# RG-LRU layer: input parts taken before the norm's root, the root multiplied in by VectorE as units leave PSUM

## The chip, the cores and the metric

The kernel runs on one core of a Trainium2 chip. The metric is the device time of one execution in microseconds (us). Engine names as in the profile: PE is TensorE's matmul, PEld its weight load, DVE VectorE, ACT ScalarE, POOL GpSimd, SP the engine that issues the DMAs.

## The reference, cut to what matters

The model has four layers: latent attention, HGRN2, RG-LRU, latent attention. Every layer computes `x + W_out(mixer(in_proj(rmsnorm(x))) * silu(gate))`. The change concerns the third layer and the norm in front of it:

```python
def rmsnorm(x, g):
    y = xf * lax.rsqrt(jnp.mean(xf * xf, axis=-1, keepdims=True) + EPS)
    return (y * g).astype(x.dtype)

def rglru_layer(h, conv_buf, h0, w_in, conv_w, conv_b, w_a, b_a, w_x, b_x, lam, w_out):
    xb, gate = jnp.split(h @ w_in, 2, axis=-1)
    y = conv_b + sum(xpad[:, j:j + s] * conv_w[j] for j in range(C_CONV))   # causal, width 4
    r = sigmoid(yh @ w_a + b_a);  i = sigmoid(yh @ w_x + b_x)               # per head, 128x128
    log_a = -C_GATE_C * r * softplus(-lam);  a = exp(log_a)
    u = sqrt(-expm1(2.0 * log_a)) * (i * y)
    hs = scan of (a, u) over time
    return (hs * silu(gate)) @ w_out
```

The root of the mean square is one number for each token, so `(x * g * root) @ w` is `((x * g) @ w) * root`.

## The kernel before, in words

Features lie on the 128 partitions, tokens (1024 of the prompt and 8 samples, 1032 columns) along the free dimension. The residual `c.x` and the normed input `c.h` are kept as 8 blocks of 128x1032. A matmul of full precision is made of three fp32r products: each operand is split into a high part (a copy by ACT) and a low part (the difference, by POOL for weights, by DVE for the input), and PE sums hi·hi, lo·hi and hi·lo.

**The stage ahead** is the output projection of layer 2 (`streamed_projection`, called through `output_projection`). Its `Norm` sums the squares of the residual while blocks finish. At the end `Norm.root` (L189) has ACT copy three residual blocks times their norm weights (L192), then take Ln (L195) and Exp (L198) of the sum: `rstd`, the root. Then comes the scaling step: `scale_first` (L200) has POOL multiply the root into those three blocks, `scale_rest` (L206) has DVE make the other five as residual times weight times root. A barrier ends the stage.

**The RG-LRU layer** first computes a decay rate from a small vector (`rglru_decay_rate`), then `rglru_heads` runs eight heads of 128 features. Each head has six units (`unit`, L2577): 0 to 2 are the recurrent branch `xb`, 3 to 5 the gate, for a third of the tokens (344 columns) each; a unit is 24 matmuls (8 blocks times 3 products). Units alternate between two PSUM banks. Unit n may start when the units up to n-2 have left PSUM, as L2579 says:

```python
wait(pe, unit_drained, NU * h + (n - 1))
```

The order on every engine is written out by hand in its `head` function, which for head h also works on head h+1 (`following`) and the first weights of head h+2 (`after`). Engines run their own list in order.
- PE: unit 0 of h+1, the two gate matrices of h (12 matmuls, L2599, on the convolved `y`), units 1 to 5 of h+1.
- ACT: high part of the gate weights of h+1 (L2615), Silu of the gate (L2633), drain of unit 0 (L2627: a copy from PSUM to `xb` or `graw`), two Sigmoids, drain 1, Exp and Tanh, drain 2, Square, drain 3, high part of the first weights of h+2, Sqrt, drains 4 and 5. Silu, Sigmoid, Exp and Sqrt each load a table first.
- DVE: waits for Square and Tanh, makes `a2` (L2741), convolution of h+1 (L2720 to L2736: seven instructions, three small copies), then waits for POOL's product, scan (L2748), small pieces for the samples.
- POOL: low part of the gate weights (L2682), gated output of h-1 (L2688), i times y (L2697), low part of the first weights of h+2, `a2` times that (L2702, which the scan waits for).

Ahead of the heads ACT splits the eight input blocks (L2668) and DVE makes their low parts (L2763); head 0's six units are drained by ACT, the high part of head 1's first weights coming after them, while DVE runs head 0's convolution as soon as three units are drained.

Of the kernel before, what the change touches and what calls it, by code (L numbers as in the profile page):

```python
# [13 lines left out]
F32 = mybir.dt.float32  # L14
F32R = mybir.dt.float32r
I32 = mybir.dt.int32
ACT = mybir.ActivationFunctionType
ALU = mybir.AluOpType
AX = mybir.AxisListType

P = 128
# [26 lines left out]
def wait(engine, sem, count):  # L48

    if not (isinstance(count, int) and count <= 0):  # L50
        engine.wait_ge(sem, count)
# [9 lines left out]
def following(layer):  # L61

    return layer + 1 if layer + 1 < LAYERS else None


class Chip:


    def __init__(self, nc, ctx, dram):
        self.nc, self.dram = nc, dram  # L70

        def sb(name, shape, dt=F32):
            return ctx.enter_context(nc.sbuf_tensor(name, shape, dt))

        self.x = sb("residual", [P, KD, T])
        self.h = sb("normed", [P, KD, T])
        self.ident = sb("ident", [P, P])
        self.ones = sb("ones", [P, P])
        self.const = sb("const", [P, len(TINY)])
        self.gains = sb("gains", [P, 4, KD])  # L80
        self.ps = ctx.enter_context(nc.psum_tensor("ps", [P, 8, 512], F32))

    def eps(self, rows=P):
        return self.const[0:rows, C_EPS:C_EPS + 1]
# [55 lines left out]
class Norm:  # L140
# [4 lines left out]

    BY_POOL = 3

    def __init__(self, c, st, layer):
        self.c, self.layer = c, layer
        self.sq = st.sb("squares", [P, 2, T])  # L150
        self.acc = st.sb("square_sums", [P, T])
        self.rstd = st.sb("rstd", [P, T])
        self.squared = st.sem("squared")
        self.accumulated = st.sem("accumulated")
        self.gain_in = st.sem("gain_in")
        self.summed = st.sem("summed")
        self.logged = st.sem("logged")
        self.rstd_ready = st.sem("rstd_ready")
# [29 lines left out]

    def root(self, act):  # L189
        nc, c = self.c.nc, self.c  # L190
        for k in range(self.BY_POOL):
            nc.scalar.activation(c.h[:, k, :], c.x[:, k, :], ACT.Copy, scale=c.gains[:, self.layer, k:k + 1]) \  # L192
              .then_inc(self.gain_in, 1)
        act.wait_ge(self.summed, 1)
        nc.scalar.activation(split_tiles(self.rstd[:, :]), c.ps[:, 0:NT, 0:TT], ACT.Ln,  # L195
                             scale=1.0 / D, bias=c.eps()).then_inc(self.logged, 1)
        act.wait_ge(self.logged, 1)
        nc.scalar.activation(self.rstd[:, :], self.rstd[:, :], ACT.Exp, scale=-0.5).then_inc(self.rstd_ready, 1)  # L198

    def scale_first(self, pool):  # L200
        pool.wait_ge(self.rstd_ready, 1)
        pool.wait_ge(self.gain_in, self.BY_POOL)
        for k in range(self.BY_POOL):
            self.c.nc.gpsimd.tensor_tensor(self.c.h[:, k, :], self.c.h[:, k, :], self.rstd[:, :], ALU.mult)

    def scale_rest(self, dve):  # L206
        c = self.c
        dve.wait_ge(self.rstd_ready, 1)
        for k in range(self.BY_POOL, KD):
            c.nc.vector.scalar_tensor_tensor(c.h[:, k, :], c.x[:, k, :], c.gains[:, self.layer, k:k + 1],  # L210
                                             self.rstd[:, :], op0=ALU.mult, op1=ALU.mult)


def streamed_projection(c, w, blocks, kt, src, drain, norm_layer=None, also_load=None, x_back=None, x_in=None):

# [4 lines left out]
    with Stage(c) as st:  # L222
# [10 lines left out]
        summed = st.sem("block_summed")  # L233
        drained = st.sem("block_drained")
        x_landed = [st.sem(f"x_landed{n}") for n in range(KD // 2)] if x_in is not None else []
        norm = None if norm_layer is None else Norm(c, st, norm_layer)
        block = st.block()
        pairs = blocks // 2

# [133 lines left out]
def split_tiles(ap):  # L373
    return ap.rearrange("p (a t) -> p a t", a=NT)


def block_of(buf, m):

    return buf[:, bass.ds(m, 1), :].rearrange("p b (a t) -> p (b a) t", a=NT)


def output_projection(c, w, kt, src, next_layer, x_back=None, x_in=None):

    streamed_projection(c, w, KD, kt, src, lambda m, psum: c.nc.vector.tensor_tensor(  # L384
        block_of(c.x, m), psum, block_of(c.x, m), ALU.add), next_layer, x_back=x_back, x_in=x_in)

# [2027 lines left out]
def hgrn_layer(c, layer):  # L2416
    with Stage(c) as st:
        out = c.x
        lb = st.sb("lb", [P, KD])
        olb = st.sb("one_less_lb", [P, KD])  # L2420
        hgrn_lower_bound(c, layer, lb, olb)
        hgrn_heads(c, out, lb, olb)
        output_projection(c, c.dram["w_hgrn_out"], KD, out, following(layer), x_in=c.dram["x_home"])

# [54 lines left out]
            step(nc.vector.tensor_scalar(p8[:, :], p[:, :], 8.0, None, op0=ALU.mult))  # L2481


def rglru_heads(c, out, m8, p8):

# [4 lines left out]
    with Stage(c) as st:  # L2492
# [118 lines left out]
        def _(act):  # L2611
# [2 lines left out]
                wait(act, unit_summed, NU * h + (3 * kind - 3))  # L2614
                nc.scalar.activation(w_hi[:, kind, :, :], ws[:, kind, :, :], ACT.Copy).then_inc(w_hi_done, 1)  # L2615

            def drain_unit(h, u, n):
                kind, t = divmod(n, 3)
                act.wait_ge(unit_summed, NU * h + (n + 1))
                if n == 0:  # L2620
                    wait(act, kept_conv, 3 * h - 3)
                    wait(act, y_parts, 7 * h - 7)
                if n == NT:
                    wait(act, og_done, h - 1)
                lo = PRE if kind == 0 else 0
                dst = (xb if kind == 0 else graw)[:, u, lo + t * TT:lo + (t + 1) * TT]
                nc.scalar.activation(dst, c.ps[:, n % 2, 0:TT], ACT.Copy).then_inc(unit_drained, 1)  # L2627

            def head(h, u, following, after):
                act.wait_ge(unit_drained, NU * h + NU)  # L2630
                if following is not None:
                    weight_hi(following, 1)
                nc.scalar.activation(graw[:, u, :], graw[:, u, :], ACT.Silu).then_inc(gs_done, 1)  # L2633
                if following is not None:
                    drain_unit(following, 1 - u, 0)
                act.wait_ge(loads, 48)
                act.wait_ge(ri_summed, 2 * h + 1)
                wait(act, m_done, h)
# [5 lines left out]
                nc.scalar.activation(split_tiles(iy[:, :]), I, ACT.Sigmoid,  # L2644
                                     bias=convw[:, bass.ds(h, 1), CONV + 2:CONV + 3].rearrange("p a k -> p (a k)")) \
                  .then_inc(i_done, 1)
                if following is not None:
                    drain_unit(following, 1 - u, 1)
                act.wait_ge(r_done, h + 1)
                wait(act, h_done, 3 * h)  # L2650
                nc.scalar.activation(a[:, :], r[:, :], ACT.Exp, scale=m8[:, bass.ds(h, 1)]).then_inc(a_done, 1)
                nc.scalar.activation(th[:, :], r[:, :], ACT.Tanh, scale=p8[:, bass.ds(h, 1)]).then_inc(th_done, 1)
                if following is not None:
                    drain_unit(following, 1 - u, 2)
                act.wait_ge(a_done, h + 1)
                nc.scalar.activation(a2[:, :], a[:, :], ACT.Square).then_inc(a2_done, 1)
                if following is not None:
                    drain_unit(following, 1 - u, 3)
                if after is not None:
                    weight_hi(after, 0)  # L2660
                act.wait_ge(m_done, h + 1)
                nc.scalar.activation(a2[:, :], a2[:, :], ACT.Sqrt).then_inc(root_done, 1)
                if following is not None:
                    drain_unit(following, 1 - u, 4)
                    drain_unit(following, 1 - u, 5)

            for kk in range(KD):
                nc.scalar.activation(h_hi[:, kk, :], c.h[:, kk, :], ACT.Copy).then_inc(h_hi_done, 1)  # L2668
                if kk == 1:
                    weight_hi(0, 0)  # L2670
            weight_hi(0, 1)
            act.wait_ge(zeroed, 1)
            for n in range(NU):
                drain_unit(0, 0, n)
            weight_hi(1, 0)
            heads(act, head)

# [33 lines left out]
        def _(dve):  # L2711
# [4 lines left out]
            def convolution(h, u):  # L2716
# [5 lines left out]
                for n in range(PRE):  # L2722
# [12 lines left out]
                nc.vector.tensor_copy(oconvs[:, bass.ds(h, 1), PRE - 1, :].rearrange("p a s -> p (a s)"),  # L2735
                                      xb[:, u, PRE + SEQ:PRE + T]).then_inc(kept_conv, 1)  # L2736

            def head(h, u, following, after):
                dve.wait_ge(a2_done, h + 1)
                dve.wait_ge(th_done, h + 1)  # L2740
                nc.vector.scalar_tensor_tensor(a2[:, :], a2[:, :], 1.0, th[:, :], op0=ALU.add, op1=ALU.mult) \  # L2741
                  .then_inc(m_done, 1)
                if following is not None:
                    convolution(following, 1 - u)
                dve.wait_ge(u_done, h + 1)
                wait(dve, og_done, h)
                wait(dve, kept_lru, 2 * h)
# [8 lines left out]
                nc.vector.tensor_copy(olrup[:, bass.ds(h, 1)], hs[:, SEQ - 1:SEQ]).then_inc(kept_lru, 1)  # L2756
                nc.vector.tensor_copy(olrus[:, bass.ds(h, 1), :].rearrange("p a s -> p (a s)"), hs[:, SEQ:T]) \
                  .then_inc(kept_lru, 1)

            nc.vector.memset(xb[:, :, 0:PRE], 0.0).then_inc(zeroed, 1)  # L2760
            for kk in range(KD):
                dve.wait_ge(h_hi_done, kk + 1)
                nc.vector.tensor_tensor(h_lo[:, kk, :], c.h[:, kk, :], h_hi[:, kk, :].bitcast(F32),  # L2763
                                        ALU.subtract).then_inc(h_lo_done, 1)
            dve.wait_ge(zeroed, 1)
            dve.wait_ge(loads, 48)
            convolution(0, 0)
            heads(dve, head)
# [2 lines left out]
def rglru_layer(c, layer):  # L2771
    with Stage(c) as st:
        out = c.h
        m8 = st.sb("m8", [P, KD])
        p8 = st.sb("p8", [P, KD])
        rglru_decay_rate(c, m8, p8)
        rglru_heads(c, out, m8, p8)
        output_projection(c, c.dram["w_rg_out"], KD, out, None)


# [149 lines left out]
```

## Time and profile before

| | |
|---|---|
| median of 3 runs | 2567.84 us (2567.36 to 2569.38) |
| the profiled execution's own time | 2569.87 us |
| its span | 2568.1 us |
| PE busy | 2306.6 us, 90% of the span |
| DVE, ACT, POOL busy | 1252.7, 1105.8, 743.6 us |
| RG-LRU layer's stage of heads | from 1484.5 us to 1737 us of the span |

Busy times overlap between engines. A stage is read from its own stretch of the span: which engine is busy throughout it, and what the others wait for.

### The profile page before, as it was taken

How to read it: one execution, taken by the hardware profiler on the slowest of the kernel's cores; microseconds unless marked ns; L12 is line 12 of the kernel's file. 1: busy time of each engine (PE TensorE's matmuls, PEld its weight loads, DVE VectorE, ACT ScalarE, POOL GpSimd, SP SyncE). 2: the span in 40 equal slices, each digit the busy share in tenths (PEclk: the TensorE clock that was granted, in tenths of full speed). 3: DMA queues.
4: the chain of work that ended last, by engine and by line, in shares of the span. 5: the costliest groups of instructions: out<-in, count | busy, mean ns of one | idle time of the engine just before them, and what ended most of it. 6: DMA issues, size and time to landing. Idle time of an engine off the chain costs nothing. (4 is left out here: it accounts for less than half of the span.)

```text
span 2568.1 us, 47717 instructions
## 1 busy us (share of the span) xinstructions
PE 2306.6 (90%) x17886; PEld 1915.2 (75%) x17886; DVE 1252.7 (49%) x1964; ACT 1105.8 (43%) x1868; POOL 743.6 (29%) x818
## 2 busy tenths in 40 slices
PE   7998999999759999999958769978899989999987
PEld 6956666666658999999947769968897566666657
DVE  4133555655343666666663236652311445655652
ACT  3065544544333555444443136662312644444431
POOL 2143322322221222222222314542111532322311
PEclk9998999999879999999958879988999999999998
DMA  4011433433221111111003011101112033433432
GB/s 151 17 44 36 118 111 103 119 99 112 99 75 75 52 52 44 52 52 52 27 11 124 8 58 38 54 2 60 66 41 83 27 98 99 121 97 107 120 126 94
DMA packets 103268, 187.59 MB, mean 73 GB/s; under 512 B 15610, under 2 KB 84220, under 8 KB 101780
## 3 DMA queue, kind: packets, MB, share of 16 engines
q1 hardware_dynamic: 103060, 184.81, 22.7%
q8 instruction: 131, 2.15, 0.4%
q14 instruction: 77, 0.63, 0.1%
HBM read 164.84 MB, written 19.92 MB: 72 GB/s over the span
## 5 line engine op out<-in xcount | busy, mean ns | idle before, releaser
L1328 POOL TENSOR_TENSOR latents_t_lo<-pages_t,latents_t_hi 128x256 fp32r<-128x256 f32 x256 | 187.1, 731 | 550.1 <-ACT latents_t_hi L1543 549.2
L1685 DVE TENSOR_REDUCE sums<-w_uq 128x8 f32<-128x512 f32 x256 | 175.1, 684 | 279.6 <-ACT w_uq L1551 279.1
L2004 PE MATMUL ps<-normed_hi,w_hi 128*128 128x344 f32 x768 | 260.9, 340 | 30.5 <-DMA g_norm<-in_hgrn_g_norm 27.2
L2004 PE MATMUL ps<-normed_hi,w_lo 128*128 128x344 f32 x768 | 251.5, 327 | 0.0
L2004 PE MATMUL ps<-normed_lo,w_hi 128*128 128x344 f32 x768 | 251.2, 327 | 0.0
L1406 PE MATMUL ps<-w_uk_hi,latents_t_hi 128*128 128x512 f32 x512 | 236.1, 461 | 10.3 <-POOL latents_t_lo L1328 10.3
L1551 ACT ACTIVATE w_uq<-ps 128x512 f32<-128x512 f32 x256 | 152.8, 597 | 213.6 <-PE ps L1406 212.6
L1406 PE MATMUL ps<-w_uk_hi,latents_t_lo 128*128 128x512 f32 x512 | 204.3, 399 | 0.0
L1406 PE MATMUL ps<-w_uk_lo,latents_t_hi 128*128 128x512 f32 x512 | 204.0, 398 | 0.0
L332 PE MATMUL ps<-src_hi,w_hi 128*128 128x344 f32 x576 | 126.0, 328 | 58.5 <-POOL w_lo L303 58.5
L2004 PEld LDWEIGHTS ps<-normed_hi,w_hi 128*128 128x128 f32 x768 | 149.7, 195 | 35.7 <-DMA g_norm<-in_hgrn_g_norm 27.8
L1560 ACT ACTIVATE latents<-ps,bias,rq 128x256 f32<-128x256 f32 (+7 forms) x128 | 106.0, 828 | 135.6 <-DVE bias L1699 121.1
L2586 PE MATMUL ps<-normed_hi,w_hi 128*128 128x344 f32 x384 | 128.0, 333 | 39.1 <-POOL w_lo L2682 36.5
L1420 PE MATMUL ps<-residual,normed 96*128 96x512 f32 (+3 forms) x384 | 155.0, 513 | 8.8 <-ACT w_uq L1551 6.2
L2252 POOL TENSOR_TENSOR normed<-normed,k 128x512 f32<-128x512 f32 x56 | 94.2, 1682 | 209.0 <-ACT normed L2135 175.9
L2004 PEld LDWEIGHTS ps<-normed_lo,w_hi 128*128 128x128 f32 x768 | 149.7, 195 | 0.5
L2004 PEld LDWEIGHTS ps<-normed_hi,w_lo 128*128 128x128 f32 x768 | 149.4, 195 | 0.0
L384 DVE TENSOR_TENSOR residual<-ps,residual 128x1032 f32 (+1 forms) x32 | 39.4, 1232 | 223.0 <-PE ps L332 223.0
L332 PEld LDWEIGHTS ps<-src_hi,w_hi 128*128 128x128 f32 x576 | 99.8, 195 | 60.3 <-POOL w_lo L303 60.3
L303 POOL TENSOR_TENSOR w_lo<-w_slots,w_hi 128x512 fp32r<-128x512 f32 (+1 forms) x32 | 62.5, 1953 | 270.3 <-ACT w_hi L272 270.3
L1406 PEld LDWEIGHTS ps<-w_uk_hi,latents_t_hi 128*128 128x128 f32 x512 | 97.4, 190 | 54.2 <-issue 34.6
L2120 ACT ACTIVATE normed<-ps 128x344 f32<-128x344 f32 x96 | 43.1, 454 | 209.1 <-PE ps L2004 209.0
(320 smaller groups left out, 5431.0 us busy)
## 6 DMA issues: line engine op xcount, KB each, us to landing
pages_t<-in_pages_t SPq DMA_DIRECT2D x256, 208.0 KB, 2.6
pages<-in_pages SPq DMA_DIRECT2D x256, 128.0 KB, 2.1
w_slots<-in_w_hgrn SPq DMA_DIRECT2D x32, 512.0 KB, 3.6
w_slots<-in_w_mla_in SPq DMA_DIRECT2D x18, 512.0 KB, 3.6
x_home<-residual SPq DMA_DIRECT2D x2, 4128.0 KB, 15.1
w_slots<-in_w_rg SPq DMA_DIRECT2D x16, 512.0 KB, 3.3
residual<-in_x SPq DMA_DIRECT2D x8, 516.0 KB, 8.2
residual<-in_x SPq DMA_DIRECT2D x1, 4128.0 KB, 13.7
```

The source lines that it names most:

```text
L303: nc.gpsimd.tensor_tensor(w_lo[:, u, :, :], ws[:, u, :, :], w_hi[:, u, :, :].bitcast(F32), ALU.subtract).then_inc(w_lo_done, 1)
L332: mm = nc.tensor.matmul(c.ps[:, NT * u + t, 0:TT], a[:, u, k, :], b[:, k, cols], start=(k == 0 and n == 0), stop=(k == kt - 1 and n == 2))
L1328: nc.gpsimd.tensor_tensor(lat_lo[:, g % DEPTH, :, :].rearrange("p k t -> p (k t)"), ring[:, g % RING, 0:KVL], lat_hi[:, g % DEPTH, :, :].r ...
L1406: mm = nc.tensor.matmul(keys(g), x[:, e, k, :], y[:, k, :], start=(n == 0), stop=(n == len(products) - 1))
L1420: mm = nc.tensor.matmul(S[:, lo:hi], c.h[0:QK, 2 * f + e, qt * P:(qt + 1) * P], c.x[0:QK, 2 * f + e, lo:hi], start=True, stop=True)
L1551: nc.scalar.activation(sq[:, g % 2, :], keys(g), ACT.Square).then_inc(squared, 1)
L1560: nc.scalar.activation(probs[:, G % 2, e, 0:n], S[:, 0:n], ACT.Exp, scale=m.rq[:, qt, 2 * f + e:2 * f + e + 1], bias=bias[:, u:u + 1], acc ...
L1685: nc.vector.tensor_reduce(ss[:, b % 2, p, :], sq[:, g % 2, :].rearrange("p (h d) -> p h d", h=H), AX.X, ALU.add).then_inc(ssum, 1)
L2004: mm = nc.tensor.matmul(bank[:, 0:TT], w[:, slot, kk, :], x[:, kk, cols], start=(kk == 0 and m == 0), stop=(kk == KD - 1 and m == 2))
L2120: nc.scalar.activation(raw[:, place, t * TT:(t + 1) * TT], bank[:, 0:TT], ACT.Copy) \
L2252: nc.gpsimd.tensor_tensor(halves(z[:, l % 2, 0:SEQ], half)[:, :, 0, :], halves(dd[:, l % 2, 0:SEQ], half)[:, :, 0, :], halves(k[:, 0:SEQ], ...
L2586: mm = nc.tensor.matmul(c.ps[:, n % 2, 0:TT], x[:, kind, kk, :], y[:, kk, t * TT:(t + 1) * TT], start=(kk == 0 and e == 0), stop=(kk == KD ...
```

## The change

The norm ahead of the RG-LRU layer is made with `scaled=False`: no copies with weights on ACT, no scaling step on POOL and DVE; the root is written into `c.h`'s last block (`c.rstd`). In `rglru_heads` the input parts are taken from `c.x` times the norm weights. The drains move from ACT to DVE and become multiplications by the root. Cut to its core:

```diff
+        self.rstd = self.h[:, KD - 1, :]
 # Norm.root, scale_first, scale_rest
-        for k in range(self.BY_POOL):
+        for k in range(self.BY_POOL if self.scaled else 0):
             nc.scalar.activation(c.h[:, k, :], c.x[:, k, :], ACT.Copy, scale=c.gains[:, self.layer, k:k + 1]) ...
+        if not self.scaled:
+            return
 # hgrn_layer
-        output_projection(c, c.dram["w_hgrn_out"], KD, out, following(layer), x_in=c.dram["x_home"])
+        output_projection(c, c.dram["w_hgrn_out"], KD, out, following(layer), x_in=c.dram["x_home"],
+                          scaled=False)
 # rglru_heads, ACT: drain_unit and all its calls go
-            def drain_unit(h, u, n):
-                nc.scalar.activation(dst, c.ps[:, n % 2, 0:TT], ACT.Copy).then_inc(unit_drained, 1)
-                nc.scalar.activation(h_hi[:, kk, :], c.h[:, kk, :], ACT.Copy).then_inc(h_hi_done, 1)
+                nc.scalar.activation(h_hi[:, kk, :], c.x[:, kk, :], ACT.Copy,
+                                     scale=c.gains[:, layer, kk:kk + 1]).then_inc(h_hi_done, 1)
             weight_hi(0, 1)
-            act.wait_ge(zeroed, 1)
-            for n in range(NU):
-                drain_unit(0, 0, n)
             weight_hi(1, 0)
 # rglru_heads, DVE
+            def drain_unit(h, u, n):
...
+                lo, cols = PRE if kind == 0 else 0, slice(t * TT, (t + 1) * TT)
+                nc.vector.tensor_tensor((xb if kind == 0 else graw)[:, u, lo + t * TT:lo + (t + 1) * TT],
+                                        c.ps[:, n % 2, 0:TT], c.rstd[:, cols], ALU.mult).then_inc(unit_drained, 1)
             def head(h, u, following, after):
+                if following is not None:
+                    drain_unit(following, 1 - u, 0)
+                    drain_unit(following, 1 - u, 1)
                 dve.wait_ge(a2_done, h + 1)
                 dve.wait_ge(th_done, h + 1)
                 nc.vector.scalar_tensor_tensor(a2[:, :], a2[:, :], 1.0, th[:, :], op0=ALU.add, op1=ALU.mult) ...
                 if following is not None:
+                    drain_unit(following, 1 - u, 2)
                     convolution(following, 1 - u)
+                    drain_unit(following, 1 - u, 3)
                 dve.wait_ge(u_done, h + 1)
...
+                if following is not None:
+                    drain_unit(following, 1 - u, 4)
+                    drain_unit(following, 1 - u, 5)
-                nc.vector.tensor_tensor(h_lo[:, kk, :], c.h[:, kk, :], h_hi[:, kk, :].bitcast(F32),
-                                        ALU.subtract).then_inc(h_lo_done, 1)
+                nc.vector.scalar_tensor_tensor(h_lo[:, kk, :], c.x[:, kk, :], c.gains[:, layer, kk:kk + 1],
+                                               h_hi[:, kk, :].bitcast(F32), op0=ALU.mult, op1=ALU.subtract) ...
             dve.wait_ge(zeroed, 1)
+            for n in range(NU):
+                drain_unit(0, 0, n)
             dve.wait_ge(loads, 48)
             convolution(0, 0)
```

The norms ahead of the other layers keep their scaling.

## Rows read from the trace of the kernel before

**Rows 1.** Busy time by stretch, with the columns and two stretches of the heads.

```profile
core 0: us, PE busy (x) PEld busy (x) DVE busy (x) ACT busy (x) POOL busy (x), PEclk, DMA share, GB/s
...
1527.00:1530.00 3.00, 3.00 (x11) 3.00 (x12) 0.00 (x0) 0.69 (x1) 2.11 (x1) 0.50 0.49 175
...
1552.00:1712.00 160.00, 160.00 (x958) 152.86 (x957) 104.59 (x103) 102.18 (x114) 87.64 (x31) 1.00 0.11 38
```

**Rows 2.** Timeline (start, length, engine, line) where the stage ahead ends.

```profile
1458.59 3.23 ACT L192 ACTIVATE normed<-residual,gains 128x1032 f32<-128x1032 f32 x3
...
1458.74 2.00 PE L185 MATMUL ps<-squares,ones 128*128 128x344 f32 x6 [0.69 <-ACT squares L163]
1461.72 1.10 ACT L195 ACTIVATE rstd<-ps,const 128x1032 f32<-128x1032 f32 x1
1462.86 1.06 ACT L198 ACTIVATE rstd<-rstd 128x1032 f32<-128x1032 f32 x1
1463.95 12.50 DVE L210 SCALAR_TENSOR_TENSOR normed<-residual,gains,rstd 128x1032 f32<-128x1032 f32 x5 [6.37 <-ACT rstd L198]
...
1476.70 0.34 SPq L2447 DMA_DIRECT2D lam<-in_rg_lam  x1
```

**Rows 3.** Timeline, splitting the input blocks ahead of the heads.

```profile
1490.66 5.82 ACT L2668 ACTIVATE normed_hi<-normed 128x1032 fp32r<-128x1032 f32 x6
...
1491.74 10.42 DVE L2763 TENSOR_TENSOR normed_lo<-normed,normed_hi 128x1032 fp32r<-128x1032 f32 x6 [3.70 <-ACT normed_hi L2668]
```

**Rows 4.** Timeline of ACT, one round of the heads.

```profile
1555.62 0.46 ACT L2627 ACTIVATE gate<-ps 128x344 f32<-128x344 f32 x1 [3.33 <-PE ps L2586]
...
1566.63 0.46 ACT L2627 ACTIVATE xb<-ps 128x344 f32<-128x344 f32 x1 [1.99 <-PE ps L2586]
...
1570.85 1.06 ACT L2656 ACTIVATE a<-a 128x1032 f32<-128x1032 f32 x1
1574.20 0.46 ACT L2627 ACTIVATE gate<-ps 128x344 f32<-128x344 f32 x1 [2.29 <-PE ps L2586]
1574.55 1.05 ACT L2615 ACTIVATE w_hi<-w_slots 128x1024 fp32r<-128x1024 f32 x1
...
1581.76 0.46 ACT L2627 ACTIVATE gate<-ps 128x344 f32<-128x344 f32 x1 [3.33 <-PE ps L2586]
```

**Rows 5.** Timeline of DVE, same round: `a2`, the convolution, the scan.

```profile
1571.94 1.23 DVE L2741 SCALAR_TENSOR_TENSOR a<-a,r 128x1032 f32<-128x1032 f32 x1 [10.47 <-ACT a L2656]
1573.09 0.81 DVE L2720 TENSOR_SCALAR y<-xb,conv_w 128x1032 f32<-128x1032 f32 x1
...
1575.24 0.22 DVE L2726 SCALAR_TENSOR_TENSOR y<-state_conv,conv_w,y 128x8 f32<-128x8 f32 x1
...
1576.81 2.37 DVE L2726 SCALAR_TENSOR_TENSOR y<-state_conv,conv_w,y 128x8 f32<-128x8 f32 x1
1579.32 3.28 DVE L2724 SCALAR_TENSOR_TENSOR y<-xb,conv_w,y 128x1024 f32<-128x1024 f32 x1
...
1582.88 2.28 DVE L2748 TENSOR_TENSOR_SCAN hs<-a,a 128x1024 f32<-128x1024 f32 x1
```

**Rows 6.** Timeline of POOL, same round: first weights of h+2, product for the scan.

```profile
1575.68 3.47 POOL L2682 TENSOR_TENSOR w_lo<-w_slots,w_hi 128x1024 fp32r<-128x1024 f32 x1 [8.54 <-ACT w_hi L2615]
1579.11 2.41 POOL L2702 TENSOR_TENSOR a<-a,i 128x1032 f32<-128x1032 f32 x1
```

**Rows 7.** Groups of DVE instructions that combine PSUM with SBUF (busy, mean ns).

```profile
L1720 DVE TENSOR_TENSOR latents<-ps,latents 128x512 f32<-128x512 f32 x16 | 11.1, 691 | 15.1 <-PE ps L1461 15.1
...
L384 DVE TENSOR_TENSOR residual<-ps,residual 128x1032 f32 x24 | 29.6, 1232 | 146.9 <-PE ps L332 146.9
```

**Rows 8.** Timeline of PE after idle times, which stand in brackets.

```profile
1526.93 0.62 PE L2586 MATMUL ps<-normed_hi,w_hi 128*128 128x344 f32 x1 [4.00 <-POOL w_lo L2682]
1527.36 0.49 PE L2586 MATMUL ps<-normed_lo,w_hi 128*128 128x344 f32 x1
...
1531.94 0.34 PE L2586 MATMUL ps<-normed_hi,w_lo 128*128 128x344 f32 x1
...
1878.07 1.23 PE L561 MATMUL ps<-src_hi,w_hi 128*128 128x344 f32 x3 [3.13 <-DVE latents L609]
```

More of the change, by code:

```diff
@@ L146, with __init__ @@
     BY_POOL = 3
-    def __init__(self, c, st, layer):
-        self.c, self.layer = c, layer
+    def __init__(self, c, st, layer, scaled=True):
+        self.c, self.layer, self.scaled = c, layer, scaled
         self.sq = st.sb("squares", [P, 2, T])
         self.acc = st.sb("square_sums", [P, T])
-        self.rstd = st.sb("rstd", [P, T])
+        self.rstd = st.sb("rstd", [P, T])[:, :] if scaled else c.rstd
         self.squared = st.sem("squared")
@@ L194, in root @@
         act.wait_ge(self.summed, 1)
-        nc.scalar.activation(split_tiles(self.rstd[:, :]), c.ps[:, 0:NT, 0:TT], ACT.Ln,
+        nc.scalar.activation(split_tiles(self.rstd), c.ps[:, 0:NT, 0:TT], ACT.Ln,
                              scale=1.0 / D, bias=c.eps()).then_inc(self.logged, 1)
         act.wait_ge(self.logged, 1)
-        nc.scalar.activation(self.rstd[:, :], self.rstd[:, :], ACT.Exp, scale=-0.5).then_inc(self.rstd_ready, 1)
+        nc.scalar.activation(self.rstd, self.rstd, ACT.Exp, scale=-0.5).then_inc(self.rstd_ready, 1)
     def scale_first(self, pool):
+        if not self.scaled:
+            return
         pool.wait_ge(self.rstd_ready, 1)
@@ L203, in scale_first @@
         for k in range(self.BY_POOL):
-            self.c.nc.gpsimd.tensor_tensor(self.c.h[:, k, :], self.c.h[:, k, :], self.rstd[:, :], ALU.mult)
+            self.c.nc.gpsimd.tensor_tensor(self.c.h[:, k, :], self.c.h[:, k, :], self.rstd, ALU.mult)
     def scale_rest(self, dve):
         c = self.c
+        if not self.scaled:
+            return
         dve.wait_ge(self.rstd_ready, 1)
@@ L210, in scale_rest, with streamed_projection @@
             c.nc.vector.scalar_tensor_tensor(c.h[:, k, :], c.x[:, k, :], c.gains[:, self.layer, k:k + 1],
-                                             self.rstd[:, :], op0=ALU.mult, op1=ALU.mult)
-def streamed_projection(c, w, blocks, kt, src, drain, norm_layer=None, also_load=None, x_back=None, x_in=None):
+                                             self.rstd, op0=ALU.mult, op1=ALU.mult)
+def streamed_projection(c, w, blocks, kt, src, drain, norm_layer=None, also_load=None, x_back=None, x_in=None, scaled=True):
     nc = c.nc
@@ L235, in streamed_projection @@
         x_landed = [st.sem(f"x_landed{n}") for n in range(KD // 2)] if x_in is not None else []
-        norm = None if norm_layer is None else Norm(c, st, norm_layer)
+        norm = None if norm_layer is None else Norm(c, st, norm_layer, scaled)
         block = st.block()
@@ L379, in block_of, with output_projection @@
     return buf[:, bass.ds(m, 1), :].rearrange("p b (a t) -> p (b a) t", a=NT)
-def output_projection(c, w, kt, src, next_layer, x_back=None, x_in=None):
+def output_projection(c, w, kt, src, next_layer, x_back=None, x_in=None, scaled=True):
     streamed_projection(c, w, KD, kt, src, lambda m, psum: c.nc.vector.tensor_tensor(
-        block_of(c.x, m), psum, block_of(c.x, m), ALU.add), next_layer, x_back=x_back, x_in=x_in)
+        block_of(c.x, m), psum, block_of(c.x, m), ALU.add), next_layer, x_back=x_back, x_in=x_in, scaled=scaled)
 class Mla:
@@ L2481, in _, with rglru_heads @@
             step(nc.vector.tensor_scalar(p8[:, :], p[:, :], 8.0, None, op0=ALU.mult))
-def rglru_heads(c, out, m8, p8):
+def rglru_heads(c, layer, out, m8, p8):
     nc, dram = c.nc, c.dram
@@ L2615, in weight_hi @@
                 nc.scalar.activation(w_hi[:, kind, :, :], ws[:, kind, :, :], ACT.Copy).then_inc(w_hi_done, 1)
-            def drain_unit(h, u, n):
[L2618 to L2626, printed above, removed]
-                nc.scalar.activation(dst, c.ps[:, n % 2, 0:TT], ACT.Copy).then_inc(unit_drained, 1)
             def head(h, u, following, after):
@@ L2633, in head @@
                 nc.scalar.activation(graw[:, u, :], graw[:, u, :], ACT.Silu).then_inc(gs_done, 1)
-                if following is not None:
-                    drain_unit(following, 1 - u, 0)
                 act.wait_ge(loads, 48)
@@ L2646, in head @@
                   .then_inc(i_done, 1)
-                if following is not None:
-                    drain_unit(following, 1 - u, 1)
                 act.wait_ge(r_done, h + 1)
@@ L2652, in head @@
                 nc.scalar.activation(th[:, :], r[:, :], ACT.Tanh, scale=p8[:, bass.ds(h, 1)]).then_inc(th_done, 1)
-                if following is not None:
-                    drain_unit(following, 1 - u, 2)
                 act.wait_ge(a_done, h + 1)
                 nc.scalar.activation(a2[:, :], a[:, :], ACT.Square).then_inc(a2_done, 1)
-                if following is not None:
-                    drain_unit(following, 1 - u, 3)
                 if after is not None:
@@ L2662, in head @@
                 nc.scalar.activation(a2[:, :], a2[:, :], ACT.Sqrt).then_inc(root_done, 1)
-                if following is not None:
-                    drain_unit(following, 1 - u, 4)
-                    drain_unit(following, 1 - u, 5)
             for kk in range(KD):
-                nc.scalar.activation(h_hi[:, kk, :], c.h[:, kk, :], ACT.Copy).then_inc(h_hi_done, 1)
+                nc.scalar.activation(h_hi[:, kk, :], c.x[:, kk, :], ACT.Copy,
+                                     scale=c.gains[:, layer, kk:kk + 1]).then_inc(h_hi_done, 1)
                 if kk == 1:
@@ L2736, in convolution @@
                                       xb[:, u, PRE + SEQ:PRE + T]).then_inc(kept_conv, 1)
+            def drain_unit(h, u, n):
+                kind, t = divmod(n, 3)
+                dve.wait_ge(unit_summed, NU * h + (n + 1))
+                if n == 0:
+                    wait(dve, kept_conv, 3 * h - 3)
+                    wait(dve, y_parts, 7 * h - 7)
+                if n == NT:
+                    wait(dve, og_done, h - 1)
+                lo, cols = PRE if kind == 0 else 0, slice(t * TT, (t + 1) * TT)
+                nc.vector.tensor_tensor((xb if kind == 0 else graw)[:, u, lo + t * TT:lo + (t + 1) * TT],
+                                        c.ps[:, n % 2, 0:TT], c.rstd[:, cols], ALU.mult).then_inc(unit_drained, 1)
             def head(h, u, following, after):
+                if following is not None:
+                    drain_unit(following, 1 - u, 0)
+                    drain_unit(following, 1 - u, 1)
                 dve.wait_ge(a2_done, h + 1)
@@ L2762, in _ @@
                 dve.wait_ge(h_hi_done, kk + 1)
-                nc.vector.tensor_tensor(h_lo[:, kk, :], c.h[:, kk, :], h_hi[:, kk, :].bitcast(F32),
-                                        ALU.subtract).then_inc(h_lo_done, 1)
+                nc.vector.scalar_tensor_tensor(h_lo[:, kk, :], c.x[:, kk, :], c.gains[:, layer, kk:kk + 1],
+                                               h_hi[:, kk, :].bitcast(F32), op0=ALU.mult, op1=ALU.subtract) \
+                  .then_inc(h_lo_done, 1)
             dve.wait_ge(zeroed, 1)
+            for n in range(NU):
+                drain_unit(0, 0, n)
             dve.wait_ge(loads, 48)
@@ L2776, in rglru_layer @@
         rglru_decay_rate(c, m8, p8)
-        rglru_heads(c, out, m8, p8)
+        rglru_heads(c, layer, out, m8, p8)
         output_projection(c, c.dram["w_rg_out"], KD, out, None)
```

## The prediction

> **What bounds the kernel now.** I read the busy times first (the table above): TensorE leads by far, but that is a mean over stages, so I went to the two stretches that the change touches. At the end of the stage ahead the timeline shows a chain with nothing beside it: PE's sums end at 1460.74, ACT's three weight copies hold Ln back to 1461.72, Exp ends at 1463.92, DVE's five scaling instructions take 12.50 us, and the next stage's first DMA goes out 0.25 us after them [rows 2]. PE is idle all that time, so an end moved forward moves everything behind it. In the heads the busy times by stretch show the reverse: PE is busy for all of 160 us at granted clock 1.00, DVE for 104.59, ACT for 102.18 [rows 1]. There other engines cost nothing until they make PE wait. The last view is PE's idle times and what its matmuls do behind them [rows 8].
>
> PE's beat in the heads: drain 3 and drain 5 start at 1574.20 and 1581.76 [rows 4], two units apart, so a unit takes 3.78 us. A drain starts 0.08 after its unit's end: units 2 to 5 end at 1570.3, 1574.1, 1577.9 and 1581.7. A round (drain 5 to drain 5) is 26.14.
>
> **The change, part by part.**
>
> Scaling step gone. Without the copies Ln can start when the sums are in, about 1460.85 for 1461.72, so 0.87 us earlier; Exp then ends at 1463.05, and the next DMA follows it by 0.25 or so instead of following DVE's end at 1476.45. The stage behind starts 13.4 us earlier (1476.70 less 1463.3) [rows 2]. No step with a DMA is moved, and SP's and POOL's queues only lose work. **-13.4**, certain to some 0.3.
>
> Splitting the input. ACT's copies take a scale, as the weight copies did: 3.23 us for three against 5.82 for six is 0.11 more each, but DVE behind them is slower anyway [rows 2, 3]. DVE's subtraction becomes a fused multiply and subtract; the fused instruction with the same shape took 1.23 us (`a2`) [rows 5], and six subtractions took 10.42 [rows 3]. Bounds 0 and 0.65 (six times 0.11); I take **+0.4**, as a pointer to a weight is added too.
>
> First head. Before, ACT splits head 1's first weights only after its six drains, and PE stands 4.00 us for the low part [rows 8]. Now the split no longer has drains ahead of it, so that wait goes. What is late next is the convolution of head 0: it was run beside units 3 to 5, and now stands behind DVE's six drains. After unit 5 come a drain, then the convolution, with one POOL instruction (low gate weights) in its middle: by the working below 0.5 + 7.6 us. PE has one unit (3.78) to run meanwhile, then waits 4.3 us for the gates. One wait replaces another of nearly the same length with the same loss of clock: **+0.4**, between -4 (POOL stays out of the convolution) and +1.5.
>
> The drains in the rounds. One drain on DVE reads PSUM and SBUF. Nothing of 344 columns of this kind stands in the rows; 512 take 691 ns and 1032 take 1232 [rows 7], 1.04 ns a column, so 344 take 0.52 us by the line through both (ACT took 0.46 [rows 4]). Its price is not the 0.52 but its place in the queue. Drains 0 and 1 stand in front of `a2`'s multiplication and cost nothing: ACT, rid of drain 1's wait of 1.99 us, of drain 1 itself and of drain 2, finishes Square about 2.9 us before its old end at 1571.91, that is near 1569.0 [rows 4], and drain 1 is over at 1567.1. The multiplication, 1.23 us, ends at 1570.3, just as unit 2 does. Drain 2 ends at 1570.9, and the convolution starts at 1571.0, 2.1 us earlier than at 1573.09 [rows 5].
>
> Behind it stands drain 3. In this round the convolution, with the small copies, runs from 1573.09 to 1582.88, 9.8 us, because POOL's two instructions fall into it: an instruction on 8 columns takes 2.37 us where its twin takes 0.22, another is stretched to 3.28 [rows 5, 6]. Both will still fall into it: the split of the weights of h+2 needs only unit 2 and goes from 1574.55 to about 1570.4, so POOL asks at 1571.5; Sqrt ends some 2.4 us after the split, and POOL asks for its product at 1573.9, both inside 1571.0 to 1580.8. So drain 3 runs from 1580.8 to 1581.35. Unit 5 uses its bank and could have started at 1577.9; it starts at 1581.4. **PE waits 3.5 us in a round** (3.2 to 3.9, if the convolution varies by 0.3). Scan and drain 4 follow while unit 5 runs (2.3 + 0.5 + 0.5 from 1581.4, over before 1585.2), so the next round's unit 0 doesn't wait, and the round is set up as before: the wait comes back each round. On ACT the waits for drain 5 shift with it and hide behind PE's next unit.
>
> The clock behind that wait. After 4.00 us of idle PE's clock is 0.50, and its matmuls last 0.49 us until 1531.94, 5.0 us long [rows 1, 8]. In that time 17.5 start, 0.287 apart, where the beat of 24 in 3.78 us would need 2.75: 2.3 us lost. An idle time of 3.13 us is followed by the same half speed (1.23 us for three) [rows 8]; 3.5 lies between the two. Bounds: 0, and 3.1 if the whole unit 5 goes at half speed (24 times 0.13). I take **2.3**.
>
> Six rounds have both POOL instructions (h = 0 to 5): 6 x (3.5 + 2.3) = **+34.8**. In the seventh there are no weights of h+2, so one stretch of about 2.15 us less: the convolution ends at 1578.6 in the same count, drain 3 at 1579.2, **+1.3**, too short an idle time for me to add clock. The last head has nothing behind it: its drain 5 is 0.06 us longer.
>
> A rule of the Trainium skill bears on this: "SBUF — State Buffer", section "Who interferes with whom", holds that a VectorE instruction with two SBUF inputs and a GpSimd instruction that reads SBUF exclude each other for the whole instruction, and that one with a single SBUF input is left alone. By it the convolution is stopped and the drains are not, which is the sum here; were the two engines only slowed a little the sum would be the rival of -12.6 below. The stretched 2.37 us speaks for the rule.
>
> Sum: -13.4 + 0.4 + 0.4 + 34.8 + 1.3 = +23.5 us. It stands against the profiled execution (own time 2569.87, span 2568.1); that lies 2.0 over the median, within what the three runs spread, so I add it to the median: 2567.84 + 23.5, about 2591.
>
> **The rivals.**
> - *DVE has room* (faster). DVE is busy 104.59 of 160 us; six drains of 0.52 a round add 3.1 to 26.14, some 12%. If POOL's instructions stayed out of the convolution it would take 9.8 - 2.15 - 2.0 = 5.65, drain 3 would be over at 1577.2, before 1577.9, and PE would not wait at all: -13.4 + 0.4 + 0.4 = -12.6, 2555 us. The point from which it decides is a convolution under 6.3 us. For it: the busy share, and every drain is short. Against: both stretches stand in the trace [rows 5, 6], and the two requests come earlier but not early enough. Chance 0.08. The Trainium skill's page "Perfetto Trace Analysis", section "Optimizing Scalar/DVE Operations", would have work moved off VectorE only when it is saturated; by that rule the drains are well placed here and this rival is the forecast. The traces show 65% and a late order, so it gets no more than the chance given.
> - *The wait without the clock.* PE waits 3.5 us six times but is granted full speed behind it: -13.4 + 0.8 + 21 + 1.3 = +9.7, 2577.5. For it: the waits are shorter than 4.00. Against: half speed after 3.13 [rows 8]. Chance 0.15, with the cases in which some rounds drop.
> - *Half the wait* (no change). POOL's product slips behind the convolution, one stretch instead of two: 1.3 us of wait in each of seven rounds, no clock: -13.4 + 0.8 + 9.1 = -3.5, 2564. Chance 0.05. That the change doesn't do what it says I see no room for: `c.h` is unused between its last reading and the root.
> - *More waits than counted.* DVE's small pieces behind the scan are stretched too (as instructions on 8 columns were) and drain 4 comes 2 us late in six rounds: about +12 more, 2603. Chance 0.05.
>
> **How the numbers follow.** The forecast case has the rest, 0.67. Its own range: 3.2 + 1.6 to 3.9 + 2.8 a round with the small terms gives +16 to +29, 2584 to 2597. To hold 8 in 10 the range takes in the case without clock and a margin above: 2576 to 2599. A measurement of this kernel tells 0.2%, about 5 us, from no change. Slower by more: forecast, the case without clock, the case of more waits, 0.87. Faster by more: the first rival, 0.08. Within: 0.05.
>
> **What would show it.** Right: the stretch from Exp to the decay rate's DMA under 0.5 us; DVE rows that read `ps` and `normed` at about 0.52; PE's first matmul of a unit 5 preceded by 3 to 4 us of idle time ended by DVE, six times, and matmuls of 0.49 behind it; PEclk below 1 in the heads; rounds of 31 to 32 us, a short one last. PE's wait for POOL at the first head replaced by one for the convolved `y`. The forecast is wrong if drain 3 starts within 3.8 us of unit 3's end, which would take a convolution that POOL doesn't stop, or if PE's matmuls keep 0.32 behind the waits.

## The result, and the profile after

The changed kernel takes **2589.34 us** in the median of four runs (2587.83 to 2591.18) against 2568.34 for the kernel before, measured beside it: ratio 1.008, 95% interval [1.0068, 1.0093]. It is 21.0 us slower. The profiled execution took 2589.28 us, its span is 2587.5. Of all executions reported below one, of *norm only*, ran slow (3859.68 us at a granted clock of 0.551, where its other three had 0.945 to 0.948), and it is left out of the numbers.

The gain where the stage ahead ends is all there. The timeline of the changed kernel (start, length, engine, line):

```profile
1457.60 2.00 PE L186 MATMUL ps<-squares,ones 128*128 128x344 f32 x6 [0.69 <-ACT squares L164]
1459.64 1.12 ACT L196 ACTIVATE normed<-ps,const 128x1032 f32<-128x1032 f32 x1 [2.09 <-PE ps L186]
1460.80 1.06 ACT L199 ACTIVATE normed<-normed 128x1032 f32<-128x1032 f32 x1
1462.11 0.34 SPq L2453 DMA_DIRECT2D lam<-in_rg_lam  x1
```

From the end of the sums to the next stage's first DMA there are 2.51 us (1459.60 to 1462.11), where [rows 2] had 15.96 (1460.74 to 1476.70): 13.45 less.

The loss is in the heads, and PE says for whom it waits. PE's waits in the layer (us in total, times, longest):

```profile
PE ps L2592 <- DVE gate L2728: 21.7, 7, 3.7
PE ps L2592 <- POOL w_lo L2663: 18.8, 1, 18.8
PE ps L2605 <- DVE y L2707: 4.0, 1, 4.0
```

L2592 is the unit's matmul, L2728 the drain on DVE: seven waits for a drain of the gate's units, one in each round, where the kernel before had none in its rounds. (The 18.8 is the idle time ahead of the first head.) One round on DVE, to be held against [rows 5]:

```profile
1530.44 0.52 DVE L2728 TENSOR_TENSOR xb<-ps,normed 128x344 f32<-128x344 f32 x1
1531.00 0.82 DVE L2701 TENSOR_SCALAR y<-xb,conv_w 128x1032 f32<-128x1032 f32 x1
1531.85 3.31 DVE L2705 SCALAR_TENSOR_TENSOR y<-xb,conv_w,y 128x1024 f32<-128x1024 f32 x1
1535.08 2.38 DVE L2707 SCALAR_TENSOR_TENSOR y<-state_conv,conv_w,y 128x8 f32<-128x8 f32 x1
...
1540.51 0.51 DVE L2728 TENSOR_TENSOR gate<-ps,normed 128x344 f32<-128x344 f32 x1
1540.93 2.28 DVE L2746 TENSOR_TENSOR_SCAN hs<-a,a 128x1024 f32<-128x1024 f32 x1
...
1543.65 0.51 DVE L2728 TENSOR_TENSOR gate<-ps,normed 128x344 f32<-128x344 f32 x1
```

Drain 2, the convolution from 1531.00 to 1540.51 with two stretched instructions, drain 3, scan, drain 4. POOL's two instructions of the same round, which run beside the stretched ones (compare [rows 6]):

```profile
1531.64 2.44 POOL L2663 TENSOR_TENSOR w_lo<-w_slots,w_hi 128x1024 fp32r<-128x1024 f32 x1 [4.53 <-ACT w_hi L2621]
1534.04 3.40 POOL L2683 TENSOR_TENSOR a<-a,i 128x1032 f32<-128x1032 f32 x1
```

And PE, whose unit 5 can start only behind drain 3:

```profile
1537.63 0.32 PE L2592 MATMUL ps<-normed_hi,w_lo 128*128 128x344 f32 x1
1541.07 0.65 PE L2592 MATMUL ps<-normed_hi,w_hi 128*128 128x344 f32 x1 [3.12 <-DVE gate L2728]
1541.52 0.49 PE L2592 MATMUL ps<-normed_lo,w_hi 128*128 128x344 f32 x1
...
1544.39 0.38 PE L2592 MATMUL ps<-normed_hi,w_lo 128*128 128x344 f32 x1
1544.61 0.32 PE L2592 MATMUL ps<-normed_hi,w_hi 128*128 128x344 f32 x1
```

3.12 us idle, then matmuls of 0.49 us for 3.3 us, then 0.32 again. The long waits of the six rounds are 3.12, 3.70, 3.60, 3.66, 3.58 and 3.12, the short one of the seventh 0.96. Over the rounds the granted clock is 0.93, where it was 1.00 [rows 1], and PE is busy for 173.3 of 192 us (the stretch, then busy us of PE, PEld, DVE, ACT, POOL, clock, DMA):

```profile
1541.00:1733.00 192.00, 173.30 (x958) 164.44 (x959) 99.14 (x138) 88.36 (x78) 76.79 (x30) 0.93 0.09 29
```

So much for what the trace shows; that the two stretched instructions and the clock are causes is for the experiments.

### The profile page after: what moved, and what is told of

It is laid out like the page before. It is cut to its first block and busy times, and to the rows that moved or that the text cites. A ratio compares the mean times of both kernels' runs of the same rounds, so it can differ in the third digit from the quotient of the medians.

```text
span 2587.5 us, 47695 instructions
## 1 busy us (share of the span) xinstructions
PE 2318.1 (90%) x17886; PEld 1923.4 (74%) x17886; DVE 1244.2 (48%) x2007; ACT 1084.2 (42%) x1817; POOL 729.2 (28%) x815
## 5 line engine op out<-in xcount | busy, mean ns | idle before, releaser
L2592 PE MATMUL ps<-normed_hi,w_hi 128*128 128x344 f32 x384 | 133.4, 347 | 43.6 <-DVE gate L2728 21.7
```

The lines of the kernel that those rows point to most:

```text
L2592: mm = nc.tensor.matmul(c.ps[:, n % 2, 0:TT], x[:, kind, kk, :], y[:, kk, t * TT:(t + 1) * TT], start=(kk == 0 and e == 0), stop=(kk == KD ...
```

## The experiments

All kernels were timed beside the kernel before (2568.84 for the first four runs, 2569.04 for the last three). Stages that no edit touches differ by up to 5 us or so from one profiled execution to another: the sums of the norm end at 1460.74 before, at 1457.21 in the run called *drains only* and at 1455.66 in the last run of the table, and what follows the last gate matmul lasts between 849.3 and 855.0 us. The table therefore also has the stretch of the heads, from the first unit's matmul to the end of the last gate matmul, in each profiled execution.

| kernel | median us | ratio, 95% interval | stretch of the heads, us |
|---|---|---|---|
| before | 2568.34 | | 222.65 |
| the change | 2589.34 | 1.008 [1.0068, 1.0093] | 258.52 |
| norm only | 2555.97 | 0.9945 [0.9925, 0.9966] | 223.74 |
| drains only | 2597.1 | 1.011 [1.009, 1.013] | 256.51 |
| shorter POOL | 2569.15 | 1.0003 [0.9994, 1.0013] | 238.71 |
| PE kept at work | 2580.29 | 1.0037 [1.0026, 1.0049] | 247.15 |
| drain 3 moved | 2584.78 | 1.0061 [1.0044, 1.0079] | 251.93 |
| drains early | 2559.82 | 0.9958 [0.9942, 0.9975] | 227.75 |
| drains early, first head too | 2551.65 | 0.9936 [0.9916, 0.9957] | 220.41 |

**The change in two halves.** First the norm alone, with the root left out:

```diff
 # the changed kernel, with ACT's and DVE's lists of the heads as before:
+                nc.scalar.activation(dst, c.ps[:, n % 2, 0:TT], ACT.Copy).then_inc(unit_drained, 1)   # on ACT
-                nc.vector.tensor_tensor(..., c.ps[:, n % 2, 0:TT], c.rstd[:, cols], ALU.mult)         # on DVE
```

> The first half of the change alone: scaling step gone and input parts from the residual times the norm weights, but the drains stay plain copies on ACT in the order of the kernel before (the root is left out). Theory: the stage behind starts 13.4 us earlier and all of it reaches the end, 2555 us. Rival (the scaling step's 12.5 us were hidden by something the next stage waits for anyway): 2568, no change.

It took 2555.97, 12.9 us less than before (8.7 to 19.3 by the interval). Its rounds, with the old order of drains, are PE's throughout:

```profile
1540.00:1700.00 160.00, 160.00 (x954) 152.41 (x953) 104.00 (x103) 102.94 (x115) 85.50 (x30) 1.00 0.12 38
```

Then the drains alone:

```diff
 # the kernel before, with ACT's and DVE's lists of the heads as in the change, and
+                nc.vector.tensor_copy((xb if kind == 0 else graw)[:, u, lo + t * TT:lo + (t + 1) * TT],
+                                      c.ps[:, n % 2, 0:TT]).then_inc(unit_drained, 1)
```

> The other half alone: the scaling step stays, the six drains go from ACT to DVE in the order of the changed kernel, as plain copies. Theory: PE waits 3.1 to 3.7 us for drain 3 in six rounds and runs the unit behind it partly at half speed, so this half costs what the change cost plus what the norm saved: 21.0 + 13.4 = 34 us, 2603. Rival (the loss comes from the multiplication by the root, or from reading another input): a few us, 2568 to 2575.

It took 2597.1, 28.3 us more than before. PE's waits in it, and a drain 3, now a copy:

```profile
PE ps L2586 <- DVE gate L2721: 21.7, 7, 3.7
```

```profile
1550.72 0.51 DVE L2721 COPY gate<-ps 128x344 f32<-128x344 f32 x1
```

The waits are those of the change, to the tenth, with no multiplication and the old input; the heads take 33.9 us more than before, as expected (34). The median came out 6 us under the expected 2603. In the profiled executions such a difference lies outside the heads: they start 3.9 us earlier than before (1489.39 for 1493.24), and what follows them is 2.9 us shorter. The multiplication itself is free: a drain takes 0.51 us as a copy and as a product. Adding the halves by the heads' stretch, 1.1 + 33.9 = 35.0 against 35.9 for the whole.

**Does POOL set the wait?**

```diff
+                nc.gpsimd.tensor_tensor(w_lo[:, kind, 0:blocks, :], ws[:, kind, 0:blocks, :],
+                                        w_hi[:, kind, 0:blocks, :].bitcast(F32), ALU.subtract)...
                 if after is not None:
-                    weight_lo(after, 0)
+                    weight_lo(after, 0, 1)
```

> The changed kernel with POOL's low part of the first weights of h+2 made for one block of eight only (seven eighths of it left out, so about 2.0 us less of POOL inside each convolution). Theory: the convolution shrinks by those 2.0 us, PE's wait for drain 3 falls from 3.5 to 1.5 us in six rounds, too short for the clock to drop: 2589.3 - 6 x (2.0 + 1.9) = 2566. If the clock still drops, 2577. Rival (drain 3's place alone costs the time, POOL is only beside it): 2589, same.

2569.15. PE's waits, and a round's clock and busy times:

```profile
PE ps L2592 <- DVE gate L2729: 10.2, 7, 1.8
```

```profile
1520.00:1706.00 186.00, 176.01 (x1029) 166.86 (x1027) 96.04 (x146) 97.34 (x87) 71.66 (x32) 0.98 0.10 33
```

Six waits of 1.17 to 1.78 us where there were 3.1 to 3.7: what POOL no longer does comes off PE's wait nearly one for one (its instruction takes 0.49 us instead of 2.4, and 21.7 less 10.2 is 11.5, or 1.9 a round). Behind four of the six the matmuls keep 0.32; behind the two longest (1.78 and 1.75 us) the clock fell after all, 1.1 and 1.4 us after PE had begun again, for some dozen matmuls of 0.49 each time. The expectation that so short a wait leaves the clock alone held four times in six. The heads shrink by 19.8 us, 11.5 of wait and 8.2 in the six units behind the waits, which run faster. The rival, that drain 3's place alone costs the time, falls; the place and POOL make it together. Only one of POOL's two instructions was shortened. The share of the other is read from the trace alone, where 8 columns take 2.38 us beside it and 0.22 without.

**Is the clock part of the loss?**

```diff
+                        if n == NU - 1 and after is not None:
+                            pe.wait_ge(r_done, h + 1)
+                            for _ in range(20):
+                                nc.tensor.matmul(c.ps[:, 2, 0:TT], w_hi[:, 1, 0, :], h_hi[:, 0, 0:TT],
+                                                 start=True, stop=True)
                         unit(following, n)
```

> The changed kernel with 20 matmuls of no use (344 columns, another PSUM bank, 3.15 us) put on PE ahead of unit 5's wait in six rounds. Theory (the clock is part of the loss): the wait stays as long, matmuls behind it keep 0.32, and six times 1.9 us come back: 2578. Rival (only the wait counts, or the half speed hides behind something): 2589, same; if the added matmuls overrun the wait, more.

2580.29, 9.1 us less than the change; the heads take 11.4 us less. PE in one round, L2613 being the matmuls of no use, and the clock over the rounds:

```profile
1568.32 3.32 PE L2613 MATMUL ps<-normed_hi,w_hi 128*128 128x344 f32 x20
1572.19 0.43 PE L2592 MATMUL ps<-normed_hi,w_hi 128*128 128x344 f32 x1 [0.55 <-DVE gate L2733]
1572.45 0.32 PE L2592 MATMUL ps<-normed_lo,w_hi 128*128 128x344 f32 x1
```

```profile
1541.00:1715.00 174.00, 172.08 (x1025) 163.23 (x1024) 92.61 (x129) 88.35 (x78) 75.74 (x29) 1.00 0.10 32
```

Unit 5 starts no sooner, 3.12 to 3.71 us behind unit 4's end as in the change, but runs at full speed in all six rounds. The clock costs 11.4 / 6 = 1.9 us on average behind each long wait.

**One drain moved, then all.**

```diff
+                    if between is not None and n in between:      # in the convolution's loop
+                        drain_unit(h, u, between[n])
-                    convolution(following, 1 - u)
-                    drain_unit(following, 1 - u, 3)
+                    convolution(following, 1 - u, {0: 3})
```

> The changed kernel with drain 3 moved into the convolution (behind its third instruction), drains 4 and 5 left behind the scan. Theory: the wait before unit 5 goes (at most 0.5 us left), but drain 4 is late next: convolution, scan and small pieces end about 3 us after unit 5, so unit 0 of the next round waits about 3 us with the same half speed behind it: 2589.3 less 0 to 10 us, 2584. Rival (drain 3 alone is the loss): 2555.

2584.78. The wait before unit 5 is gone and the next one is there. DVE's drains 4 and 5 behind the scan, and PE's unit 0 of the next round:

```profile
1541.68 0.93 DVE L2730 TENSOR_TENSOR gate<-ps,normed 128x344 f32<-128x344 f32 x2
```

```profile
1542.33 0.42 PE L2592 MATMUL ps<-normed_hi,w_hi 128*128 128x344 f32 x1 [2.19 <-DVE gate L2730]
```

In the change drain 4 was hidden by the late unit 5. Six waits of 2.1 to 2.9 us take the place of six of 3.1 to 3.7, and behind five of them the matmuls fall to 0.49 us again. So the other two drains have to move as well:

```diff
-                    convolution(following, 1 - u)
-                    drain_unit(following, 1 - u, 3)
+                    convolution(following, 1 - u, {0: 3, 2: 4})
+                    drain_unit(following, 1 - u, 5)
...
-                if following is not None:                         # behind the scan
-                    drain_unit(following, 1 - u, 4)
-                    drain_unit(following, 1 - u, 5)
```

> The changed kernel with drain 3 behind the convolution's third instruction, drain 4 behind its last, drain 5 ahead of the scan; nothing else. Theory: no drain is queued longer than one unit, PE's waits in the rounds fall under 0.5 us each and the clock stays: 2589.3 - 6 x (3.5 + 1.9) - 0.7 = 2556. Rival (DVE has too much to do in a round, whatever the order): still above 2575.

2559.82, faster than before. PE's waits for drains, and its clock over the rounds:

```profile
PE ps L2592 <- DVE gate L2730: 1.2, 4, 0.4
```

```profile
1530.00:1700.00 170.00, 168.84 (x1004) 160.04 (x1003) 126.67 (x141) 92.78 (x83) 86.44 (x31) 1.00 0.11 35
```

DVE does the same work, the clock is 1.00 and PE is busy but for 1.2 us. The rival, that DVE has too much to do, falls. POOL's instructions still stretch the convolution here, but not a drain that runs inside one of them:

```profile
1549.95 2.45 POOL L2669 TENSOR_TENSOR normed<-hs,gate 128x1032 f32 x1 [0.50 <-DVE hs L2754]
1550.12 0.52 DVE L2730 TENSOR_TENSOR xb<-ps,normed 128x344 f32<-128x344 f32 x1 [0.18 <-issue]
```

That is the distinction which the Trainium skill makes ("SBUF — State Buffer", section "Who interferes with whom"), and the traces agree: 0.52 us for the drain with one SBUF input, 2.38 for 0.22 where both inputs lie in SBUF. (For copies within SBUF it doesn't hold as the forecast put it; see the last head below.)

Against *norm only* the heads still take 4.0 us more. Of these, 2.5 are in the rounds (159.3 us for the last six, from drain 5 to drain 5, against 156.8), where PE restarts behind waits of up to 0.4 us. Another 1.3 are at the first head, where PE still stands for the convolution, and its gates run at half speed:

```profile
1518.60 6.78 PE L2605 MATMUL ps<-y,w_gates 128*128 128x344 f32 x12 [4.05 <-DVE y L2707]
```

```diff
-            for n in range(NU):
+            for n in range(NT):
                 drain_unit(0, 0, n)
             dve.wait_ge(loads, 48)
-            convolution(0, 0)
+            convolution(0, 0, {0: 3, 2: 4})
+            drain_unit(0, 0, 5)
```

> As early, and head 0's convolution goes behind its first three drains, with drains 3 and 4 inside and 5 behind. Theory: PE's idle time of 4.0 us ahead of the gates of head 0 goes, and so does its loss of clock (gates took 5.19 us instead of 3.44): 4.0 + 1.8 us less than early, 2550, faster than both kernels. Rival (another wait takes its place, such as for low weights): as early.

2551.65 us, 0.9936 of the kernel before and the lowest median of all. That is 8.2 us less than *drains early*, where 5.8 had been expected from the gates' 5.19 us in the change; in *drains early* they had taken 6.78. The gates of head 0 in it:

```profile
1509.40 3.63 PE L2605 MATMUL ps<-y,w_gates 128*128 128x344 f32 x12
```

No idle time stands in front and they run at full speed. The heads take 220.41 us, 2.2 less than before. From the first unit's matmul to unit 1 of head 1 there are 38.06 us where the kernel before had 43.02, as its wait of 4.00 us [rows 8] and the half speed behind it are gone; the rounds give 2.5 of that back.

## Why the prediction was right, step by step

The forecast was +23.5 us, the measurement +21.0, inside the forecast case's own range (+16 to +29). By the stretches that the edit touches it is -13.45 and +35.87, together +22.4; the rest is in stages that it doesn't touch. By steps:

- *Scaling step, -13.4.* 13.45 by the timelines. *Norm only* shows that it reaches the end: 12.9 (8.7 to 19.3).
- *Splitting the input, +0.4.* DVE's six fused instructions take 10.55 us against 10.42 [rows 3]. The start of the heads costs more, for a reason the sum lacked: PE waits about 2.5 us for the last low part in both kernels, and the half speed behind it lasted longer this time, 5.78 us from drain 0 to drain 1 instead of 4.31. Head 0's six units take 31.4 us for 29.7 (29.8 in *drains only*, with the old splitting; 30.4 to 31.5 in the other runs, with the new one), so the term was 1.3 us too small.
- *First head, +0.4.* The wait for low weights went and the one for the convolution came, 4.05 for 4.00 us, by the order that was named: six drains, then a convolution stretched by one POOL instruction. In the change the gates took 5.19 us behind it. From the end of head 0's units to unit 1 of head 1 there are 12.6 us for 13.3, so 0.7 less where 0.4 more was forecast. This term and the one before came to +1.0 together for +0.8: each was off, and that they cancel is luck.

```profile
1509.86 0.52 DVE L2728 TENSOR_TENSOR gate<-ps,normed 128x344 f32<-128x344 f32 x1 [3.27 <-PE ps L2592]
...
1512.34 2.33 DVE L2707 SCALAR_TENSOR_TENSOR y<-state_conv,conv_w,y 128x8 f32<-128x8 f32 x1
```

- *A drain's price, 0.52.* 517 and 512 ns.
- *The wait in six rounds, 3.5 each.* 3.12 to 3.70, mean 3.46. The convolution started 0.56 us after drain 2 did (1530.44 to 1531.00; 0.6 by the price of a drain) and was stretched twice, and *shorter POOL* shows for one of POOL's two instructions that it is the cause of its part of the wait.
- *The clock, 2.3 each.* Mis-sized: 1.9 by *PE kept at work*. The term took one stretch of half speed of 5.0 us for all; the six lasted 3.0 to 5.9. Over six rounds that is 2.4 us too much, about what the forecast is high by, but the untouched stages differ by as much, so that this match shows nothing.
- *The seventh round, +1.3.* 0.96 us, no half speed behind it.
- *The last head, 0.06.* Nothing was lost there, but by luck. Drain 5 is late, behind the scan and a small copy that POOL's gated output of head 6 stretched:

```profile
1731.96 2.40 DVE L2755 COPY o_lru_s<-hs 128x8 f32<-128x8 f32 x1
1734.27 0.92 DVE L2728 TENSOR_TENSOR gate<-ps,normed 128x344 f32<-128x344 f32 x2
1735.23 1.06 ACT L2627 ACTIVATE gate<-gate 128x1032 f32<-128x1032 f32 x1 [11.93 <-DVE gate L2728]
```

But ACT's Silu, which waits for it, starts 1.8 us after the unit's end in both kernels (1735.23 for an end near 1733.5; 1714.22 for 1712.4), as in the kernel before a table load stood in its way and here the table was in already. The copy of 2.40 has a single SBUF input, so the rule was put too simply in the forecast; the Trainium skill ("SBUF — State Buffer", section "Who interferes with whom") excepts copies that can run in one of VectorE's faster modes with two ports. From the end of the last gate matmul to the next stage's first weight DMA there are 21.74 us before and 21.68 after.

The rival *DVE has room* rested on busy shares. *Drains early* shows that it described the engine rightly and the change wrongly: DVE does have the room, but the list it works through in order didn't use it. The section that the rival named from the Trainium skill ("Perfetto Trace Analysis", "Optimizing Scalar/DVE Operations") says when moving work off a saturated VectorE may make sense; it doesn't say that an engine with room takes more in any order, which is what the rival needs. Another sentence of it comes nearer: where unsaturated engines cause bubbles on others, breaking up instructions may let work end sooner. Here no instruction was broken up, but drains put between the convolution's instructions brought the heads from 258.52 to 227.75 us. The case *wait without the clock* falls with the rounds' clock of 0.93. *Half the wait* falls with the waits themselves, over 3 us in six rounds, and *more waits than counted* as no unit 0 waits in the rounds of the change.

## What to carry to other kernels

When work moves to another engine, ask first where it stands in that engine's list and what it releases, then what it costs: 0.06 us more for a drain was nothing, and standing behind a 9.5 us convolution cost PE 33 us (21.7 of waiting, 11.4 of clock). An instruction that frees a buffer belongs where the buffer is next needed, if need be in the middle of another step, and moving one alone only shows the next one that is late. A row of instructions that such a wait hangs on is priced at the length that it has in the trace beside the other engines' work, not at its undisturbed length. And an idle time of PE is priced together with the half speed that can follow it.

## What the runs showed of the hardware that was not expected

The clock after nearly equal idle times varies: in the change, behind 3.70 us the half speed lasted 5.9 us, behind 3.66 us 3.0, and behind one of the waits of 3.12 the matmuls ran at full speed for another 1.0 us before it fell. In *shorter POOL* waits of 1.2 to 1.7 us never lowered it and those of 1.75 and 1.78 did, over 1 us after PE had begun again. In *drain 3 moved* a wait of 2.19 us didn't lower it and one of 2.11 did. Why this varies was not tried.
